# Second scan of a two-layer hybrid trunk: early coefficients, reordered buffers and staging, 64-byte parts

## The reference

```python
proj = h @ w_in                                    # q, k, v, z, beta_logit, a_logit
qkv = silu(causal_depthwise_conv(qkv, conv_w))     # 4 taps, 1040 columns
m   = where(strict, (k*beta) @ k.T * decay, 0)     # per head and chunk of 64
sol = triangular_solve(m, [v*beta, k*beta*exp(g)], unit_diagonal=True)   # u, w
# over the chunks, in order:
v_new = u_c - w_c @ s
o = q_c @ s + a_c @ v_new
s = s * tot + k_c.T @ v_new
# after them
h = h + (headnorm(o) * silu(z)) @ w_out
return rms_norm(h)[:, 16:]
```

## Time and profile before

| | us |
|---|---|
| median of three runs | 1447.57 (1446.95 to 1448.4) |
| the profiled execution, its time | 1450.41 |
| its span | 1448.5 |
| TensorE busy | 1423.2 |
| VectorE, ScalarE, GpSimd busy | 757.0, 466.1, 412.3 |

### The profile page before, as it was taken

One profiled execution on the slowest core, in us unless ns is written; L12 is line 12 of the kernel. 1 busy time (PEld: TensorE's weight loads), 2 busy tenths in 40 slices (PEclk: granted clock), 3 DMA queues, 4 the chain that ended last, 5 costly groups with the idle time before them and its releaser, 6 DMA issues.

```text
span 1448.5 us, 21451 instructions
## 1 busy us (share of the span) xinstructions
PE 1423.2 (98%) x8458; PEld 1198.8 (83%) x8458; DVE 757.0 (52%) x937; ACT 466.1 (32%) x958; POOL 412.3 (28%) x359
## 2 busy tenths in 40 slices
PE   8999999999999999999999999999989999999997
PEld 6878799878888899999999999888866777777776
DVE  5225522225553366455465687799934654444442
ACT  5325621133222253433334544321232622111121
POOL 3213134251110131122121177243342541222200
PEclk9999999999999999999999999999999999999999
DMA  5621244466554135444463232244378885555530
GB/s 191 187 81 58 76 153 150 157 235 198 182 175 142 47 88 128 110 109 122 121 197 98 76 92 79 83 125 137 117 262 208 237 230 154 145 141 158 167 88 29
DMA packets 213918, 200.35 MB, mean 138 GB/s; under 512 B 62873, under 2 KB 177065, under 8 KB 213570
## 3 DMA queue, kind: packets, MB, share of 16 engines
q1 hardware_dynamic: 207234, 187.53, 43.6%
q10 hardware_dynamic: 6592, 11.54, 2.9%
HBM read 131.93 MB, written 67.09 MB: 137 GB/s over the span
## 4 chain that ended last, share of the span: by engine, by line
PE 55%; DVE 6%; ACT 2%; DMA 1%; issue 1%; DVEq 0%; POOLq 0%; ACTq 0%; POOL 0%
PE banks L2195 17%; PE banks L3011 13%; PE banks L2272 12%; DVE gdn L2529 4%; PE banks L3067 2%; PE banks L3100 2%; PE banks L3072 2%; PE banks L2089 2%; PE banks L3081 1%; PE banks L2113 1%; PE banks L3055 1%; PE banks L3024 1%; DMA gdn_z<-gdn 1%; ACT gdn L2328 1%; ACT gdn L2350 1%
## 5 line engine op out<-in xcount | busy, mean ns | idle before, releaser
L2195 PE MATMUL banks<-hn_hi,gdn 128*128 128x352 f32 x1488 | 309.6, 327 | 0.0
L2195 PEld LDWEIGHTS banks<-hn_hi,gdn 128*128 128x128 f32 x1488 | 244.5, 188 | 4.4 <-issue 2.7
L2195 PE MATMUL banks<-hn_lo,gdn 128*128 128x352 f32 x744 | 168.1, 321 | 0.0
L2272 PE MATMUL banks<-gdn,hn_hi 128*128 128x512 f32 x512 | 165.1, 403 | 1.8 <-ACT gdn L2475 1.5
L2529 DVE SCALAR_TENSOR_TENSOR gdn<-gdn,conv_taps,gdn 128x1040 f32<-128x1040 f32 x96 | 161.7, 1684 | 7.7 <-ACT gdn L2336 4.9
L2480 POOL TENSOR_TENSOR gdn<-gdn,gdn 128x1024 fp32r<-128x1024 f32 x31 | 84.4, 2722 | 268.4 <-ACT gdn L2311 268.4
L2195 PEld LDWEIGHTS banks<-hn_lo,gdn 128*128 128x128 f32 x744 | 127.3, 188 | 0.0
L920 PE MATMUL banks<-gdn,hn_hi 128*128 128x512 f32 x384 | 120.5, 395 | 0.0
L2272 PEld LDWEIGHTS banks<-gdn,hn_hi 128*128 128x128 f32 x512 | 96.7, 190 | 28.1 <-issue 3.0
L2272 PE MATMUL banks<-gdn,hn_lo 128*128 128x512 f32 x256 | 102.2, 399 | 0.0
L3011 PE MATMUL banks<-gdn,gdn 128*128 128x512 f32 x384 | 95.4, 397 | 1.4 <-DVE gdn L3226 1.2
(11 more groups left out here) (321 smaller groups left out, 2404.0 us busy)
## 6 DMA issues: line engine op xcount, KB each, us to landing
gdn<-in_gdn_w_in SPq DMA_DIRECT2D x32, 512.0 KB, 4.0
gdn<-in_x SPq DMA_DIRECT2D x16, 512.0 KB, 3.5
gdn<-in_gla_w_in SPq DMA_DIRECT2D x32, 256.0 KB, 4.2
gdn_kq<-gdn SPq DMA_DIRECT2D x16, 512.0 KB, 3.8
gdn_v<-gdn SPq DMA_DIRECT2D x16, 512.0 KB, 3.5
gdn<-in_gdn_w_in SPq DMA_DIRECT2D x32, 256.0 KB, 4.5
gdn<-gdn_kq SPq DMA_DIRECT2D x16, 512.0 KB, 3.8
gdn<-gdn_ek SPq DMA_DIRECT2D x16, 512.0 KB, 5.5
```

Of the source, the lines that this page charges most:

```text
L2195: return pe.matmul(acc[n % 2][:, b, 0:m], w[n % 2][:, kt, :], x[:, kt, PAD + s:PAD + s + m], start=(kt == 0 and e == 0), stop=(kt == KT - ...
L2272: mm = pe.matmul(z_bank(grp * TT + t), x[:, kt, P + t * P:P + (t + 1) * P], z_half(w, p_), start=(kt == 0 and e == 0), stop=(kt == KT - 1 ...
```

## The change

1. The second scan's coefficients: those of chunks 0 and 1 are stored by two DMAs of 256 KB into a DRAM tensor of their own (gdn_ua_first), as soon as `weigh` is done. Chunk 0's are loaded from it, and only then the whole of `sc` is stored. The meta system is multiplied by beta on GpSimd right behind its inverse. SyncE starts the scan's loads when the inverse has ended, ahead of `weigh`, with values ahead of the rows of w_out.
2. Buffers: what is loaded before the full store is done (the state, vn, ua, kt, h[1]) lies over the scratch, and what comes later (transposed outputs, z, h[0]) over `sc`. The last group of z has four slots. One row of w_out has its high part in a hole of D words.
3. Staging: ua(1) and v(1) are loaded ahead of rows 2 and 3, row 4 in chunk 0. GpSimd scales the meta keys before it decays chunk 0.
4. The last output projection has banks 0 and 1 and does not wait for `residual` of the tile before.
5. Parts of type float32r start at multiples of 64 bytes (LINE words), as do the arena, hn and A_DEC (80 words, 72 before); the spans are 352, 352 and 336 columns.

The diff with its context left out (`steps` is moved as it is and not shown):

```diff
...
-SPANS = [(0, 352), (352, 344), (696, 344)]
+SPANS = [(0, 352), (352, 352), (704, 336)]
...
 def gla(nc, S, T, A, H, bank, x, meta, norm_w, w_in, w_gk, b_gk, head_norm, w_out, next_norm):
-    with nc.sbuf_tensor("gla", [P, ARENA - A_DEC], F32), nc.Block() as block:
+    with nc.sbuf_tensor("gla", [P, ARENA + LINE - GH * 2 * NT], F32), nc.Block() as block:
...
     def row(self, offset):
         def take(shape, dt=F32):
-            at = row.end
-            row.end = at + -(-math.prod(shape[1:]) // 8) * 8
+            size = math.prod(shape[1:])
+            unit = LINE if dt == F32R else 8
+            at = -(-row.end // unit) * unit
+            row.end = at + -(-size // 8) * 8
...
+LINE = 16
-A_DEC = GH * 2 * NT
+A_DEC = -(-GH * 2 * NT // LINE) * LINE
...
+        sc_x = sc[:, 0:2 * C * C].rearrange("p (j x) -> p j x", x=2 * C)
+        FIRST = 2
...
         def z_slot(k):
-            return k % 4 if k < G3 * TT else 1 + k % 2
+            return k % 4
         def z_stored(eng, k):
-            if k < G3 * TT:
-                eng.wait_ge(S(f"ni_z_out{k % 4}"), 16 * (k // 4 + 1))
-            else:
-                eng.wait_ge(S(f"ni_zl_out{k % 2}"), 16 * ((k - G3 * TT) // 2 + 1))
+            eng.wait_ge(S(f"ni_z_out{k % 4}"), 16 * (k // 4 + 1))
...
-            sp.wait_ge(S("ni_u"), 4)
+            sp.wait_ge(S("ni_um"), 1)
-            sp.dma_start(T.gdn_ua, sc[:, 0:2 * C * C].rearrange("p (j x) -> p j x", x=2 * C)).then_inc(S("ni_ua_out"), 16)
+            sp.wait_ge(S("ni_inv"), steps(C))
+        def store_first(sp):
+            sp.wait_ge(S("ni_u"), 2)
+            for c in range(FIRST):
+                sp.dma_start(T.gdn_ua_first[c], sc_x[c::NCH]).then_inc(S("ni_ua_out"), 16)
+        def store_ua(sp):
+            sp.dma_start(T.gdn_ua, sc_x).then_inc(S("ni_ua_out"), 16)
         def store_z(sp, k):
-              .then_inc(S(f"ni_z_out{k % 4}" if k < G3 * TT else f"ni_zl_out{k % 2}"), 16)
+              .then_inc(S(f"ni_z_out{k % 4}"), 16)
...
-            elif k < G3 * TT:
+            else:
-            elif k < G3 * TT + 2:
-                z_stored(act, G3 * TT - 4 + z_slot(k))
-            else:
-                z_stored(act, k - 2)
...
+                pool.wait_ge(S("ni_minv"), steps(NMETA))
+                pool.tensor_tensor(m_rows, m_rows, bc(m_g[:, 1, :].rearrange("p (j o) -> p j o", o=1),
+                                                      [NH, NMETA, NMETA]), ALU.mult).then_inc(S("ni_um"), 1)
...
-                dve.wait_ge(S("ni_minv"), steps(NMETA))
-                dve.tensor_tensor(m_rows, m_rows, bc(m_g[:, 1, :].rearrange("p (j o) -> p j o", o=1),
-                                                     [NH, NMETA, NMETA]), ALU.mult).then_inc(S("ni_u"), 2)
...
+        F.store_first, F.store_ua, F.ua_first, F.ua_all = store_first, store_ua, 16 * FIRST, 16 * (FIRST + 1)
...
-        St = behind.take([P, NH, NDV])
-        kq_at, ek_at, St_at = 0, 2 * NH * 2 * C, ahead.end
+        og = [behind.take([P, HP, NDV]) for n in range(2)]
+        h = [behind.take([P, D])]
+        hole = behind.end
+        behind.end = FRONT + 2 * C * C
+        assert behind.end == hole + D
+        kq_at, ek_at, St_at = 0, 2 * NH * 2 * C, behind.end
+        St = behind.take([P, NH, NDV])
-        og = [behind.take([P, HP, NDV]) for n in range(2)]
+        ua = [behind.take([P, HP, 2, C]) for n in range(2)]
-        ua = [behind.take([P, HP, 2, C]) for n in range(2)]
-        h = [behind.take([P, D]) for n in range(2)]
+        h.append(behind.take([P, D]))
-        rows_hi = [A.at(at, [P, KT, P], F32R) for at in places]
-        rows_lo = [A.at(at + D, [P, KT, P], F32R) for at in places]
-        rows_raw = [A.at(at + D, [P, KT, P]) for at in places]
+        rows_hi = [A.at(at if at + 2 * D <= ARENA else hole, [P, KT, P], F32R) for at in places]
+        places = [at + D if at + 2 * D <= ARENA else at for at in places]
+        rows_lo = [A.at(at, [P, KT, P], F32R) for at in places]
+        rows_raw = [A.at(at, [P, KT, P]) for at in places]
...
-        assert first_row + 2 * D * (KO - KT) <= ARENA
+        assert first_row + (2 * (KO - KT) - 1) * D <= ARENA
...
-        pY = [bank[:, 6 + n, :] for n in range(2)]
+        def pY(t, half):
+            return bank[:, (6 if t < TT - 1 else 0) + half, :]
...
-                    src = T.gdn_ua.rearrange("(h p c) j x -> p c j h x", p=2, c=NCH)[:, m]
+                    if m < 2:
+                        src = T.gdn_ua_first.rearrange("c (h p) j x -> p c j h x", p=2)[:, m]
+                    else:
+                        src = T.gdn_ua.rearrange("(h p c) j x -> p c j h x", p=2, c=NCH)[:, m]
...
             def load_meta():
+                tokens(sp, vm, T.gdn_v, 0, NMETA, RM, S("ns_in_m"))
+                keys(ktm, 0, NMETA, RM, S("ns_in_m"))
+                sp.wait_ge(S("ni_uam_out"), 16)
-                tokens(sp, vm, T.gdn_v, 0, NMETA, RM, S("ns_in_m"))
-                keys(ktm, 0, NMETA, RM, S("ns_in_m"))
...
             def chunk(m):
-                if m + 1 < NCH:
-                    load_ua(m + 1)
-                    if 1 <= m < NCH - 2:
+                if m:
+                    if m + 1 < NCH:
+                        load_ua(m + 1)
+                    if m < NCH - 2:
-                if m + 1 < NCH:
+                if 0 < m < NCH - 1:
+                    load_rows(4)
...
-                    for k in range(F.tiles + TT - 2, F.tiles + TT):
+                    for k in range(F.tiles + TT - 4, F.tiles + TT):
...
-            sp.wait_ge(S("ni_uam_out"), 16)
+            F.store_first(sp)
+            sp.wait_ge(S("ni_ua_out"), F.ua_first)
+            load_ua(0)
+            F.store_ua(sp)
+            load_ek(1)
-            sp.wait_ge(S("ni_ua_out"), 16)
-            load_ua(0)
-            load_ek(1)
+            sp.wait_ge(S("ni_ua_out"), F.ua_all)
+            load_ua(1)
+            load_v(1)
-            load_rows(2, 3, 4)
+            load_rows(2, 3)
...
             def out_project(t):
-                wait(pe, S("ns_yd"), 2 * t)
+                if t < TT - 1:
+                    wait(pe, S("ns_yd"), 2 * t)
...
-                                mm = pe.matmul(pY[half].rearrange("p (a b) -> p a b", b=P), o,
+                                mm = pe.matmul(pY(t, half).rearrange("p (a b) -> p a b", b=P), o,
...
-            act.wait_ge(S("ni_ua_out"), 16)
+            act.wait_ge(S("ni_ua_out"), F.ua_all)
...
-                dve.tensor_tensor(h[t % 2][:, c], pY[half], h[t % 2][:, c], ALU.add).then_inc(S("ns_yd"), 1)
+                dve.tensor_tensor(h[t % 2][:, c], pY(t, half), h[t % 2][:, c], ALU.add).then_inc(S("ns_yd"), 1)
...
-            dve.wait_ge(S("ni_ua_out"), 16)
...
-            decayed(0)
-            pool.wait_ge(S("ns_kqd"), 1)
+            decayed(0)
+            pool.wait_ge(S("ns_kqd"), 1)
...
 def gdn(nc, S, E, T, A, H, bank, w_in, w_out, head_norm, out_norm, out):
-    with nc.sbuf_tensor("gdn", [P, ARENA + 8], F32), nc.Block() as block:
+    with nc.sbuf_tensor("gdn", [P, ARENA + LINE], F32), nc.Block() as block:
...
+        T.gdn_ua_first = dram("gdn_ua_first", [2, NH, C, 2 * C])
...
-            base = -(-nc.sbuf_base // 32) * 32
-            sb("hn", [P, 2 * KT * TP + 8], F32, hctx)
+            base = -(-nc.sbuf_base // (4 * LINE)) * 4 * LINE
+            sb("hn", [P, 2 * KT * TP + LINE], F32, hctx)
-            A, E = Arena(nc, -(-nc.sbuf_base // 32) * 32), Sems(nc)
+            A, E = Arena(nc, -(-nc.sbuf_base // (4 * LINE)) * 4 * LINE), Sems(nc)
```

More of the change, by code:

```diff
@@ L2468, in z_out, with steps @@
                 act.wait_ge(S("ni_vtr"), 3 * (NV // P))
-            elif k < G3 * TT:
+            else:
                 z_stored(act, k - 4)
-            elif k < G3 * TT + 2:
-                z_stored(act, G3 * TT - 4 + z_slot(k))
-            else:
-                z_stored(act, k - 2)
             act.activation(zs[z_slot(k)], z_bank(k), ACT.Silu).then_inc(S("ni_zev"), 1)
+        def steps(size):
+            n, s = 0, 2
+            while 2 * s <= size:
+                n += 2 * (2 * s - 1) if s <= 8 else size // (2 * s) * (1 + 4 * (s // (4 if s == 32 else s // 2)))
+                s *= 2
+            return n
         def gpsimd(pool):
@@ L2679, in weigh @@
                                       bc(beta[:, r, :], [P, 32, c.stop - c.start]), ALU.mult).then_inc(S("ni_u"), 1)
-                dve.wait_ge(S("ni_minv"), steps(NMETA))
-                dve.tensor_tensor(m_rows, m_rows, bc(m_g[:, 1, :].rearrange("p (j o) -> p j o", o=1),
-                                                     [NH, NMETA, NMETA]), ALU.mult).then_inc(S("ni_u"), 2)
-            def steps(size):
-                n, s = 0, 2
-                while 2 * s <= size:
-                    n += 2 * (2 * s - 1) if s <= 8 else size // (2 * s) * (1 + 4 * (s // (4 if s == 32 else s // 2)))
-                    s *= 2
-                return n
             dve.memset(xs[:, 0:CONV - 1], 0.0).then_inc(S("ni_xs_zero"), 1)
```

## The result

The changed kernel takes 1438.07 us (median of 4 runs, 1436.69 to 1438.57) against 1447.99 of the kernel before beside it (4 runs); the ratio is 0.9929, with an interval of 0.9912 to 0.9946. Run again on another chip it came to 1438.06 (5 runs), ratio 0.993 [0.9917, 0.9943]. So some 10 us are gained (0.7%), where 22.7 were forecast, and the time lies 2 us above the forecast range.

The account below looks back on a forecast made before the run. TensorE was taken as the bound, busy 1423 of 1448.5 us, losing time to stands, half clock or slow matmuls. 3.9 + 5.1 + 1.3 + 12.4 = 22.7 us from the median 1447.6 gave 1425.0; range of 8 in 10: 1420 to 1436.

Parts of the forecast that it names:

- Part 6: Matmuls across the kernel: operands on 64 bytes and spans 352/352/336 make them faster; 12.4 us, bounds 1 and 15.
- Rival A: Placement on 64 bytes does nothing (0 to 1 us), the L920 pattern coming from the piece; 1437 us, chance 0.10.
- 1, coefficients apart: Join before the second scan: separate coefficients, store order and four z slots return 3.9 of 4.4 us of stand.
- 2, the clock: Behind the join: with a stand of only 0.6 us, the clock stays up and the whole 5.1 us returns.
- 3 and 4, what moves behind the large store: Second scan: later transfers cost 0 (bounds 0 and 10 us); GpSimd's meta product and key scaling move at nothing.
- Rival C: Slower than before: SyncE stands at the full store, z and v(1) land late, chunks 1 to 3 pay; 1452, chance 0.05.
- 5, own banks: Last projection: its first matmul no longer waits 1.2 us for VectorE's sum over tile 6; 1.3 us with the restart.

Follow-up runs that it names:

- before_place: The kernel before with the placement alone (parts of the arena on 64 bytes, arena on 256; old spans, order and banks): 1440.38 us, ratio 0.9945.
- store_all_first: The changed kernel with the store of all coefficients issued right behind the two small ones, ahead of chunk 0's loads: 1449.89 us, ratio 1.001.
- no64: The changed kernel with parts of the arena on 8 words again (LINE = 8) and the old spans 352/344/344: 1441.79 us, ratio 0.9957.
- best1: The changed kernel with the arena 128 bytes later, old spans, and the next chunk's values loaded straight behind its coefficients and keys: 1434.09 us, ratio 0.9894.
- mb2: Second bench, TensorE alone: matmul groups by distance from moving to stationary operand, other column counts and spans; 227.2 to 234.3 ns at multiples of 32 bytes.
- mb1: First bench, TensorE alone: 64 groups of 24 matmuls over 8 starts of each operand, then old and new spans; fast groups lie on two diagonals.
- diff0_oldspans: The changed kernel with the arena 128 bytes later and the old spans 352/344/344: 1435.94 us, ratio 0.9902.
- diff0: The changed kernel with the arena 128 bytes later and nothing else: 1440.38 us, ratio 0.9938.
- oldspans: The changed kernel with the old spans and nothing else: 1438.39 us, ratio 0.9929.
- pair_behind_z21: best1 with SyncE waiting for the store of z of tile 21 before it stores the first pair of coefficients: 1436.8 us, ratio 0.9918.
- late_v: The changed kernel with the values of chunk 3 loaded behind two more rows of weights: 1437.9 us, ratio 0.9933.

## Why the prediction was too low

By the median 12.8 us of the 22.7 did not come. Part 6 is 9.6 of them (12.4 less 2.8), the way from one execution to the median 2.7, and the small differences of the other terms the rest. Rival A's time, 1437, is near the measured one, but its reason, that place has no part in it, is refuted by the benches and by before_place.

**1, coefficients apart.** Right in place, and in size: 3.9 us forecast, 3.64 measured. store_all_first shows that the order does it. That the size fits so well is in part luck: two steps inside were off and cancelled. The loads ahead of the pair were done sooner (pair at 1057.81, not 1061), and the pair took 7.8 us, not 5. And the four slots, on which I let the first two gaps depend, were not needed.

**2, the clock.** Mechanism right: no window under 1.00, and 4.72 us behind the join in the profiled execution where 5.1 was taken. The size was wrong for the median: that execution had lost more than most. Of the 49 executions of the kernel before beside the experiments that took 1446.7 to 1454.1 us, the 24 with a granted clock of 0.998 or more took 1447.3 (median), the 14 with 0.996 or less 1450.2. I took the sum of an execution of 1450.4 from a median of 1447.6 and called the difference the run's own. It goes with the granted clock: the spans of the two profiled executions differ by 12.6 us, the medians by 9.9. That is 2.7 us of the miss. That the join is where the other executions keep their clock is likely, but not shown, as only one execution of the kernel before has a trace.

**3 and 4, what moves behind the large store.** Cost nothing, as said, but the margins were misjudged. Rival C gave z and v(1) some 9 us, and for what comes behind them I had only the idle stretch from 1130. For the values of chunk 3 VectorE then waited 5.4 us and was done 0.6 us before TensorE asked. My evidence was a window with a share of 0.15, and after the change that window is at 1.03. I read idle transfers of the old order as slack of the new one.

**5, own banks.** Right: 1.3 forecast, 1.43 in the trace of the changed kernel.

**6, 64 bytes.** This is the step that failed: 12.4 us forecast, 2 to 4 measured (2.8 by the stages, 2.1 and 3.7 by no64). The rows were right, their cause was not. The step took an operand's own place modulo 64 bytes for what sets a matmul's time, and the benches show that it is the distance of the two operands modulo 256. The earlier trace rows each show two groups that differ in the moving operand's place modulo 64 and, with the other operand fixed, in its distance modulo 256: 160 and 192 bytes there, 160 and 0 here. One pair can't tell these apart. The earlier trace rows should have warned me: both parts off 64 bytes were faster than one off, which the 64-byte rule doesn't give and the distance does. I named that under rival A and held A at 0.10. Also, come from the last tile, whose transposed outputs have their low half elsewhere, so that every third matmul is at 128 bytes or 32 in place of 0 or 160. By them a matmul on two parts in the arena had 2.5 ns to gain; in the other seven tiles it takes 228.7 ns before and 228.8 after, and the 1.0 us taken for L3011 there was not to be had. The change put L920 and L2272 at a distance of 128, at 232.4 ns, and only L1303 at 0. L1303 gained 6.2 ns each in place of 4.1, but L2272 1.0 in place of 4.1, L920 lost 1.0 on average, and the stage of L2195, for which the sum had 2.5 us of its matmuls and most of the spans' 3.0, gained 0.55.

Even the right placement would not have brought 12.4 us: of the 8.9 us by which best1 reaches the last z group earlier than the changed kernel (1051.01 against 1059.91), 2.2 go into the stand at the join and 3.1 into the clock behind it.

By the Trainium skill, "TensorE: Matmul & The Clock Gate", section Step-by-step: what each phase is for, TensorE reads SBUF through two independent ports, one for each operand. The traces here agree for 320 and 336 columns, and not for 512: there the time depends on the two starts together (227.2 to 234.3 ns). The same page of the Trainium skill, section Back-to-back issue gap, gives a matmul alone 2.5 ns more than a column per cycle, by which an estimate for 512 columns is 215.8 ns, and about 131 ns in a sustained stream. No stream of float32r here comes near the second figure, and the lowest, 226.7, is above the first.

## What to carry to other kernels

When a pair of rows differs in one operand's address, list both operands' addresses for every line before a rule is made of it, and measure the grid by itself: two short benches settled what single pairs of rows had suggested wrongly. A gain ahead of a join is worth only what the join lets through: follow the second chain (here VectorE's inverse, the stores, SBUF still being read) to its own end. And a sum made from one profiled execution is to be taken from that execution's time, unless the term that varies between executions is known.

## What the runs showed of the hardware

- 24 matmuls of 512 columns (fp32r, 128x128 stationary) take 227.2 ns each where the stationary operand starts 0 bytes behind the moving one modulo 256, 228.8 at 192, and 232.4 to 234.3 at the other multiples of 32; 226.7 at 16 bytes (mb2; mb1 has 226.7 to 228.3, 228.8 to 229.1 and 232.0 to 234.4). With rows that lie in strided parts (L3011 from hn) 192 gave 231.5, which stays unexplained, as does the mechanism itself: that the distance decides is shown, why it does is not.
- The three spans 352/344/344 took 466.9 to 479.3 ns a triple in mb2, by distance. In the kernels' steady stretches (the first triple behind other work left out) it is 474.9 before and 472.6 in diff0_oldspans, where the bench has 477.0 and 466.9 at the same distances. So of the bench's 10 ns between these placements 2 arrive, and 0.9 us of 744 triples where the bench had 7.5; why is open. The new spans come out as in the bench: 473.7 ns in the changed kernel (bench 473.1) and 477.7 in diff0 (478.2). The 480 and 483 ns in what was expected of oldspans are not the steady times.
- Two stores of 256 KB from 8 partitions each took 7.8 to 8.7 us in packets of 32 KB, beside other transfers, and 9.8 in packets of 512 bytes.
- A stand of 2.6 us at the join, ahead of matmuls of 16 rows, brought the half clock in best1, and one of 4.3 us in pair_behind_z21; stands of 1.2 us elsewhere and of 0.94 us in late_v did not.
- One and the same kernel does not lose its clock alike in every execution: the kernel before ran with mean granted clocks of 0.994 to 0.999, and took 1446.7 to 1454.1 us.
